# Three gate pairs instead of two computed during the last head, with the branch splits placed among the last two gate slabs

## The chip, the cores and the metric

The kernel runs on one core of a Trainium2 chip. The metric is the device time of one execution in microseconds (us), as a median of several runs. PE is TensorE, the matmul engine (PEld its weight loads), DVE is VectorE, ACT is ScalarE, POOL is GpSimd, SP is SyncE, whose queue issues the loads. Each engine has its own instruction stream, which it works off in order; they meet in semaphores.

## The reference

Two transformer blocks, one after the other, on 512 tokens of width 1024, in 32-bit floats. The place of this change is the end of the first block's mixer:

```
u = rmsnorm(x, norm_mix_g);  proj = u @ w_in        # q, k, v, z of 8 delta-rule heads, fq, fk, fv of 8 attention heads,
                                                    # gate_a and gate_b, 1024 columns each
y_a = branch_a @ w_proj_gdn                         # branch_a: the 8 delta-rule heads, normed and gated, 1024 wide
y_b = branch_b @ w_proj_fox                         # branch_b: the 8 attention heads, 1024 wide
merged = sigmoid(gate_a) * y_a + sigmoid(gate_b) * y_b
h = x + merged @ w_out
x = h + square(relu(rmsnorm(h) @ w_up)) @ w_down
```

The second block has the same ending (retention and windowed attention as branches, biases on the gates, a merge, an output projection, a gated MLP).

## The kernel before, in words

Activations lie transposed: features on the 128 partitions, 512 tokens along a row. A tensor of 1024 features is 8 tiles of 128x512, numbered k. Weights come as 302 **slabs** of 1024x128 (512 KB), each of which gives 128 output features: `load_slab` on SP's queue into one of four slots, `split_hi` on ACT (rounded to the fast matmul type), `split_lo` on POOL (the remainder, in two pieces), and `slab_products` on PE: for each k three matmuls of 128x512, high by high, high by low, low by high (lines 284 to 286), 24 for a slab, all into one bank of PSUM. Both factors need the two parts, so activations are split in the same way.

`ORDER` is an order written out by hand for one round of the heads, a list of tokens that every engine walks: `s3.1` is part k=1 of the round's slab 3, `e3` is the emptying of slab 3's bank by DVE (times the row of norms), the others are stages of the head before. At `sj.0` ACT and POOL split slab j+2 (`LEAD = 2`). Rounds 1 to 7 are a loop. The last round, `LAST`, has no next head to project, so it carries the stages of head 7 and, spread among them, 2 x `AHEAD` = 4 gate slabs: gate_a and gate_b for merge tiles 0 and 1. Their 32 parts are dealt out over the 56 places of a full round. They go to buffers that the heads don't need any more (`gates_ahead`).

Then comes the merge, `merge_tiles`: a tile m makes 128 output features of `merged`. The first `AHEAD` tiles are written out and have two slabs each (j = 2, 3: the two branch projections, into banks bA and bB); the others are a loop and have four (j = 0, 1: the two gates, then the branches). PE waits before j = 2 of every tile until DVE has taken both branch results of the tile before (`branch_taken`, 2q+1). ACT takes the tanh of the ready gates and splits the slabs two ahead, both behind a wait for the tile before (`merged`).

Before the merge the two branches must be split as well. ACT waits for `branches_done`, a one-column instruction of DVE behind the last head's results, then copies 16 tiles to the high parts (`branches_hi`, line 540); DVE subtracts 16 times (`branches_lo`, line 546). The first tile's first two slabs wait for these slice by slice:

```
for k in range(KT):
    if first:
        pe.wait_ge(sem("br_lo"), 2 * KT * rnd + 2 * k + j - 1)
    slab_products(pe, ph, i, slabs[j], (bA, bB)[j - 2][:], (a_hi, b_hi)[j - 2], (a_lo, b_lo)[j - 2], ks=(k,))
```

The second block does the same with `ORDER2`, a last round of 8 gate slabs (`AHEAD2 = 4`) and four merge tiles with ready gates.

Of the kernel before, what the change touches and what calls it, by code (L numbers as in the profile page):

```python
# [23 lines left out]
F32 = mybir.dt.float32  # L24
F32R = mybir.dt.float32r

P = 128
T = 512
NT = T // P
D = 1024  # L30
KT = D // P
EPS = 1e-6
HEADS = 8
# [5 lines left out]
DVE_STEPS, LATE_STEPS = 26, 10  # L39
LEAD = 2  # L40

AHEAD = 2
AHEAD2 = 4
RET_HEADS = 4
FF2_TILES = 22
# [88 lines left out]
def program(nc, dram, out):  # L134
    order = slab_order()

    ph_heads = Phase(7, HEADS)
    ph_gates = Phase(2 * AHEAD, 1, ph_heads)
# [17 lines left out]
    with ExitStack() as ctx:  # L156
# [55 lines left out]
        gains = small("gains", [P, 5, KT])  # L212
        sq_sum = small("sq_sum", [P, T])
        r_row = small("r_row", [P, T])
        r_diag = small("r_diag", [P, NT, P])
        ms_col = small("ms_col", [P, NT])
        r_col = small("r_col", [P, NT])
        head_gain = small("head_gain", [P, 3])
# [8 lines left out]
        def sem(name):  # L227
            if name not in sems:
                sems[name] = ctx.enter_context(nc.semaphore(name))
            return sems[name]  # L230
# [101 lines left out]
        head.at = 183 * KiB  # L332
        rawq = [head(f"raw_qkv{n}", [P, 3 + T]) for n in range(3)]
        raw_fq, raw_fk, raw_fv = [head(f"raw_{n}", [P, T]) for n in ("fq", "fk", "fv")]
        gates_ahead = [rawq[0][:, 3:3 + T], rawq[1][:, 3:3 + T], rawq[2][:, 3:3 + T], raw_fq[:], raw_fk[:], raw_fv[:]]

        pre = Bump(80 * KiB, 112 * KiB)
        x_tok = pre("x_tok", [P, NT, D])
# [35 lines left out]
        LAST, places, part = [], [n for n, t in enumerate(ORDER) if is_slab(t)], 0  # L374
        for n, t in enumerate(ORDER):
            if n in places:
                if (places.index(n) + 1) * 2 * AHEAD * KT // len(places) > part:
                    LAST.append(f"s{part // KT}.{part % KT}")
                    if part % KT == 0 and part:
                        LAST.append(f"e{part // KT - 1}")  # L380
                    part += 1
            elif t not in LATE and not is_evac(t):
                LAST.append(t)
        LAST.append(f"e{2 * AHEAD - 1}")
        FIRST = [t for t in ORDER if is_slab(t) or is_evac(t) or t in LATE]
        FIRST.remove("tq")
# [145 lines left out]

        merge_g = mtmp

        def branches_hi(act, rnd):

            act.wait_ge(sem("branches_done"), rnd + 1)
            for k in range(KT):
                for hi, br in ((a_hi, br_a), (b_hi, br_b)):
                    act.copy(hi[:, k, :], br[:, k, :]).then_inc(sem("br_hi"), 1)  # L540

        def branches_lo(dve, rnd):
            for k in range(KT):
                for n, (hi, lo, br) in enumerate(((a_hi, a_lo, br_a), (b_hi, b_lo, br_b))):
                    dve.wait_ge(sem("br_hi"), (rnd * KT + k) * 2 + n + 1)
                    dve.tensor_tensor(lo[:, k, :], br[:, k, :], hi[:, k, :].bitcast(F32), ALU.subtract)\  # L546
                        .then_inc(sem("br_lo"), 1)


        def gates_before(rnd, m):  # L550
# [28 lines left out]
            merge_tiles(pe, phs, rnd, tile)  # L579

        def merge_act(act, phs, rnd):
            branches_hi(act, rnd)

            def tile(ph, i, slabs, m, ahead):
                q = rnd * KT + m
                if ahead:
                    if rnd == 0:
                        act.wait_ge(s_taken, 7 * HEADS + 2 * m + 2)
                    else:
                        act.wait_ge(sem("taken2"), ph_kv.n + 8 * (RET_HEADS - 1) + 2 * m + 2)  # L590
                    act.wait_ge(sem("merged"), 3 * q + 1)
                    for j in range(2):
                        src = gates_ahead[2 * m + j] if rnd == 0 else h_res[:, 2 * m + j, :]
                        act.activation(merge_g[j][:], src, ACT.Tanh, scale=0.5).then_inc(sem("gate_tanh"), 1)
                        split_hi(act, ph, i, slabs[2 + j] + LEAD)
                    if rnd == 1 and m == AHEAD2 - 1:
                        act.wait_ge(sem("gate_tanh"), 2 * q + 2)
                        act.dma_start(h_res[:].rearrange("p k t -> p (k t)"), h_store[:, :]).then_inc(sem("ld_x"), 16)
                    return
                for j in range(4):  # L600
                    split_hi(act, ph, i, slabs[j] + LEAD)
                    if j < 2:
                        act.wait_ge(sem("gate_taken"), gates_before(rnd, m) + j + 1)
                        act.activation(merge_g[j][:], merge_g[j][:], ACT.Tanh, scale=0.5).then_inc(sem("gate_tanh"), 1)  # L604
            merge_tiles(act, phs, rnd, tile)
# [228 lines left out]
        def ret_rounds(eng, per_round):  # L834

            per_round(FIRST2, ph_kv, 0, None)
            with eng.Fori(0, RET_HEADS - 1) as i:
                per_round(ORDER2, ph_ret, i, i)
            per_round(ORDER2, ph_gates2, 0, RET_HEADS - 1)

        L_BANKS = [(bC, bD), (bE, bF)]

# [125 lines left out]
        def ret_act(act):  # L968
# [7 lines left out]
            def per_round(tokens, ph, i, c):  # L976
# [62 lines left out]
                def ev(a_):  # L1039
                    act.wait_ge(sem("att_t_ps"), 2 * c + a_ + 1)  # L1040
                    act.copy(br_b[:, bass.ds(2 * c + a_, 1), :].rearrange("p a t -> p (a t)"), bB[:])\
                        .then_inc(sem("att_out"), 1)
# [3 lines left out]
                for a_ in range(2):  # L1046
                    stages[f"swa{a_}"] = lambda a_=a_: swa(a_)
                    stages[f"ev{a_}"] = lambda a_=a_: ev(a_)
                for u in range(4):
                    stages[f"E{u}"] = lambda u=u: softmax(u)  # L1050
                    stages[f"T{u}"] = lambda u=u: probs_t(u)
# [5 lines left out]
        def ret_dve(dve, step):  # L1057
# [10 lines left out]
            def per_round(tokens, ph, i, c):  # L1068
# [124 lines left out]
                def on2(a_):  # L1193
                    dve.wait_ge(sem("o2_ps"), 4 * c + 2 * a_ + 2)
                    dve.wait_ge(sem("att_inv"), 4 * c + 2 * a_ + 2)
                    if a_ == 0:
                        dve.wait_ge(sem("sp_ps"), 3 * c + 3)
                    else:
                        dve.wait_ge(sem("att_t_ps"), 2 * c + 1)
                    dve.tensor_tensor(a_out[:].rearrange("p (m d) -> p m d", d=64),  # L1200
                                      bA[:].rearrange("p (m d) -> p m d", d=64),
                                      rd2[:].rearrange("p n u -> p (n u)").unsqueeze(2).to_broadcast([P, 2 * NT, 64]),
                                      ALU.mult).then_inc(sem("att_scaled"), 1)
# [5 lines left out]
                for a_ in range(2):  # L1209
                    stages[f"ra{a_}"] = lambda a_=a_: rota(a_)  # L1210
                    stages[f"on{a_}"] = lambda a_=a_: on2(a_)
                for u in range(4):
                    stages[f"lg{u}"] = lambda u=u: logits(u)
                    stages[f"M{u}"] = lambda u=u: sums(u)
# [9 lines left out]
                    assert step.n == RET_STEPS, step.n  # L1224
            ret_rounds(dve, per_round)
            step.straight(start[0] + RET_HEADS * RET_STEPS)
            dve.wait_ge(sem("ret_out"), 2 * RET_HEADS)
            dve.wait_ge(sem("att_out"), 2 * RET_HEADS + 1)
            dve.tensor_scalar(ms_col[:], ms_col[:], 1.0, None, ALU.mult).then_inc(sem("branches_done"), 1)

        def ret_pool(pool):
            def per_round(tokens, ph, i, c):
# [135 lines left out]
            ffn_pool(pool)  # L1368

        def after_heads_dve(dve, step):  # L1370
            dve.wait_ge(sem("oa"), HEADS)
            dve.wait_ge(sem("ob"), HEADS)
            dve.tensor_scalar(ms_col[:, 0:1], ms_col[:, 0:1], 1.0, None, ALU.mult).then_inc(sem("branches_done"), 1)
            branches_lo(dve, 0)
            merge_dve(dve, (ph_merge0, ph_merge1), 0)
            out_dve(dve, ph_out1, 1, 32)
            mlp_dve(dve)
            ret_dve(dve, step)
            branches_lo(dve, 1)
            merge_dve(dve, (ph_merge2a, ph_merge2), 1, bias_gate)  # L1380
            out_dve(dve, ph_out2, 3, 48)
            ffn_dve(dve)
# [284 lines left out]
        def _(act):  # L1667
# [11 lines left out]
            def head_round(tokens, i, c):  # L1679
# [112 lines left out]
                for n in range(NT):  # L1792
                    stages[f"E{n}"] = lambda n=n: probs(n)
                    stages[f"T{n}"] = lambda n=n: probs_t(n)
                    stages[f"O{n}"] = lambda n=n: outs(n)
                run(tokens, stages, slab, None)

            head_rounds(act, head_round)
# [4 lines left out]
        def _(dve):  # L1803
# [15 lines left out]
            def head_round(tokens, i, c):  # L1819
# [5 lines left out]
                def evac(j):  # L1825
                    dst = (rawq[0], rawq[1], rawq[2], raw_fq, raw_fk, raw_fv, raw_z)[j]
                    dst = dst[:, 3:3 + T] if j < 3 else dst[:]
                    dve.wait_ge(s_used, ph.index(ph_i, j) + 1)
                    if c is not None and j == 5:
                        dve.wait_ge(sem("fvt_ps"), c + 1)  # L1830
                    dve.tensor_tensor(dst, slab_bank(i, j)[:], r_row[:], ALU.mult).then_inc(s_taken, 1)

# [219 lines left out]
                def probs(i_):  # L2052
# [7 lines left out]
                          "gates1": gates1, "gates2": gates2, "cola": cola, "colb": colb, "colh": colh, "dif": dif,  # L2060
                          "bd": bd, "dm": dm, "qd": qd, "fk": fk, "kpd": kpd, "vp": vp_, "kk": kk, "qk": qk, "z0": z0,
                          "xt": xt, "vk": vk, "osq": osq, "on": on_, "oa": oa}
                for x in range(4):
                    stages[f"sl{x}"] = lambda x=x: silu(x)
                for x in range(3):
# [159 lines left out]
```

## Time and profile before

| | us |
|---|---|
| median of 3 runs | 2073.38 (2070.56 to 2073.69) |
| the profiled execution | 2072.55 |
| its span in the trace | 2070.8 |
| PE busy in it | 1995.8 |
| granted TensorE clock, mean | 0.99 |

The span is measured in the trace, from the first to the last instruction; the device time of the same execution has 1.75 us around it. Matmuls overlap in the records: one of 128x512 is shown as about 390 ns, and the next starts some 230 ns after it, so paces are read from start to start. "issue" as a releaser means that the profile shows nothing for which the engine waited.

### The profile page before, as it was taken

What the parts mean: (1) busy time and instruction counts of PE and PEld (TensorE: products, weight loads), DVE (VectorE), ACT (ScalarE), POOL (GpSimd) and SP (SyncE); (2) the same over time, 40 slices, a digit from 0 to 9 for tenths busy, and PEclk for the clock granted to TensorE, in tenths of its full rate; (3) what the DMA queues carried; (4) which work ended last, traced back from release to release, by engine and by line L of the source; (5) the groups of instructions that cost most, each with busy time, mean ns of one, the idle gap of its engine ahead of it and who ended that gap; (6) DMA issues with size and microseconds to landing.
All of it is one profiled execution on the core that took longest, in us unless ns stands there. A gap on an engine that the chain in (4) does not pass through costs nothing.

```text
span 2070.8 us, 29716 instructions
## 1 busy us (share of the span) xinstructions
PE 1995.8 (96%) x11060; PEld 1630.5 (79%) x11060; DVE 909.3 (44%) x1578; ACT 691.5 (33%) x1390; POOL 929.1 (45%) x711
## 2 busy tenths in 40 slices
PE   6999999999989999999999999999989999999997
PEld 5788778887768888888888777777768888888886
DVE  4666776667642222121212355655642324335143
ACT  4333333333342223332324343444332233223222
POOL 3443344434425456444445533333325456545455
PEclk9999999999999999999999999999999999999998
DMA  5111111111113252333323321121124323323332
GB/s 184 62 62 53 57 42 61 61 51 51 61 42 106 87 176 92 102 93 101 101 91 93 112 81 61 61 61 61 51 72 133 110 72 102 111 82 93 101 102 71
DMA packets 50646, 174.25 MB, mean 84 GB/s; under 512 B 6544, under 2 KB 7312, under 8 KB 50320
## 3 DMA queue, kind: packets, MB, share of 16 engines
q1 hardware_dynamic: 50432, 171.20, 25.8%
q10 hardware_dynamic: 144, 2.10, 0.3%
q8 instruction: 47, 0.77, 0.1%
q14 instruction: 23, 0.19, 0.0%
HBM read 169.08 MB, written 4.19 MB: 84 GB/s over the span
## 4 chain that ended last, share of the span: by engine, by line
PE 88%; DVE 7%; ACT 2%; issue 2%; DMA 0%; POOL 0%; DVEq 0%; POOLq 0%; ACTq 0%; SPq 0%
PE bank L284 25%; PE bank L286 24%; PE bank L285 24%; PE bank L1458 3%; PE bank L1447 2%; PE bank L1441 2%; PE bank L944 1%; PE bank L1640 1%; DVE att_neg_max L1182 1%; PE bank L1627 1%; DVE ret_g_raw L1157 1%; PE bank L914 1%; DVE branch_a_lo L546 0%; DVE decay_b L1938 0%; DVE att_logits L1178 0%
## 5 line engine op out<-in xcount | busy, mean ns | idle before, releaser
L273 POOL TENSOR_TENSOR slab_lo<-slab_raw,slab_hi 128x512 fp32r<-128x512 f32 x604 | 821.5, 1385 | 1015.5 <-ACT slab_hi L266 1015.4
L284 PE MATMUL bank<-u_hi,slab_hi 128*128 128x512 f32 x1584 | 658.4, 416 | 17.9 <-POOL slab_lo L273 13.5
L286 PE MATMUL bank<-u_hi,slab_lo 128*128 128x512 f32 x1584 | 622.3, 393 | 0.0
L285 PE MATMUL bank<-u_lo,slab_hi 128*128 128x512 f32 x1584 | 621.2, 392 | 0.0
L266 ACT CAST slab_hi<-slab_raw 128x1024 fp32r<-128x1024 f32 x302 | 314.1, 1046 | 231.6 <-PE bank L286 230.6
L284 PEld LDWEIGHTS bank<-u_hi,slab_hi 128*128 128x128 f32 x1584 | 300.2, 189 | 80.3 <-issue 18.2
L286 PEld LDWEIGHTS bank<-u_hi,slab_lo 128*128 128x128 f32 x1584 | 299.3, 189 | 65.1
L285 PEld LDWEIGHTS bank<-u_lo,slab_hi 128*128 128x128 f32 x1584 | 300.7, 190 | 53.9 <-issue 1.7
L284 PE MATMUL bank<-hidden_hi,slab_hi 128*128 128x512 f32 x432 | 168.4, 390 | 0.3
L285 PE MATMUL bank<-hidden_lo,slab_hi 128*128 128x512 f32 x432 | 168.1, 389 | 0.0
L286 PE MATMUL bank<-hidden_hi,slab_lo 128*128 128x512 f32 x432 | 168.1, 389 | 0.0
L482 DVE TENSOR_TENSOR residual<-residual,bank 128x512 f32<-128x512 f32 x48 | 33.0, 688 | 200.6 <-PE bank L286 200.6
L284 PEld LDWEIGHTS bank<-hidden_hi,slab_hi 128*128 128x128 f32 x432 | 81.1, 188 | 18.4 <-DVE residual L1326 1.6
L286 PEld LDWEIGHTS bank<-hidden_hi,slab_lo 128*128 128x128 f32 x432 | 81.1, 188 | 16.8
L285 PEld LDWEIGHTS bank<-hidden_lo,slab_hi 128*128 128x128 f32 x432 | 81.1, 188 | 16.7
L634 DVE SCALAR_TENSOR_TENSOR mtmp<-mtmp,bank 128x512 f32<-128x512 f32 x32 | 22.0, 688 | 138.6 <-PE bank L286 138.6
L1291 ACT ACTIVATE tmp<-tmp 128x512 f32<-128x512 f32 x22 | 13.9, 632 | 177.7 <-DVE tmp L1312 177.7
L284 PE MATMUL bank<-branch_a_hi,slab_hi 128*128 128x512 f32 x128 | 52.7, 412 | 10.1 <-issue 8.4
L604 ACT ACTIVATE mtmp<-mtmp 128x512 f32<-128x512 f32 x20 | 12.6, 632 | 145.9 <-DVE mtmp L623 86.0
L765 DVE SCALAR_TENSOR_TENSOR tmp<-bank,r_row 128x512 f32<-128x512 f32 x32 | 22.1, 692 | 85.0 <-PE bank L286 85.0
L1326 DVE TENSOR_TENSOR residual<-residual,bank 128x512 f32<-128x512 f32 x24 | 16.5, 688 | 94.8 <-PE bank L286 94.8
L736 ACT ACTIVATE tmp<-tmp 128x512 f32<-128x512 f32 x32 | 20.2, 632 | 110.1 <-DVE tmp L765 110.1
(342 smaller groups left out, 2727.4 us busy)
## 6 DMA issues: line engine op xcount, KB each, us to landing
slab_raw<-slabs SPq DMA_DIRECT2D x302, 512.0 KB, 3.5
residual<-x_t SPq DMA_DIRECT2D x2, 1024.0 KB, 7.2
x_tok<-x SPq DMA_DIRECT2D x1, 2048.0 KB, 12.7
residual<-x_t SPq DMA_DIRECT2D x1, 2048.0 KB, 8.9
residual_store<-residual SPq DMA_DIRECT2D x1, 2048.0 KB, 8.7
residual<-residual_store ACTq DMA_DIRECT2D x1, 2048.0 KB, 8.1
out_t<-residual SPq DMA_DIRECT2D x8, 256.0 KB, 2.1
cos_ret<-cos_r SPq DMA_DIRECT2D x1, 256.0 KB, 3.7
```

Source lines behind the costliest of these rows:

```text
L266: act.copy(w_hi[s][:], raw[s][:]).then_inc(s_hi, 1)
L273: ins = pool.tensor_tensor(w_lo[s][:, ks, :], raw[s][:, ks, :], w_hi[s][:, ks, :].bitcast(F32), ALU.subtract)
L284: pe.matmul(bank, w_hi[s][:, k, :], x_hi[:, k, :], start=first, stop=False)
L285: pe.matmul(bank, w_hi[s][:, k, :], x_lo[:, k, :], start=False, stop=False)
L286: mm = pe.matmul(bank, w_lo[s][:, k, :], x_hi[:, k, :], start=False, stop=last)
L482: ins = dve.tensor_tensor(h_res[:, m, :], h_res[:, m, :], bank[:], ALU.add)
L634: dve.scalar_tensor_tensor(out=merge_g[j][:], in0=merge_g[j][:], scalar=1.0, in1=(bA, bB)[j][:], op0=ALU.add, op1=ALU.mult).then_inc(sem(" ...
L765: dve.scalar_tensor_tensor(out=tmp[j % 2][:], in0=bank_slab[j % 2][:], scalar=0.0, in1=r_row[:], op0=ALU.max, op1=ALU.mult).then_inc(sem(" ...
L914: mm = pe.matmul(L_BANKS[u][b // 2][:, at_ + (P if b == 0 else 0):at_ + 2 * P], a_q[a_][half, b * P:(b + 1) * P], k_cur[half, k0:(b + 1) * P],
L1441: mm = pe.matmul(out_[:, c], lhs[:, c], rhs[:, c], start=start, stop=stop)
L1447: mm = pe.transpose(out_[:, c], in_[:, c], ident[:])
L1458: mm = pe.matmul(out_[r, c], lhs[r, c], rhs[r, c], start=True, stop=True)
```

## The change

`AHEAD` goes from 2 to 3, so that three pairs of gate slabs are computed in the last round, and three merge tiles are written out with two slabs each; the loop has five turns in place of six. The list of slabs in memory follows. `SPREAD = 4` keeps the first four gate slabs on the places that they had; gate slabs 4 and 5 stand behind the emptying of the fourth, and among their sixteen parts stand eight new tokens `br0` to `br7`. Each is one k of the branch splits: two copies on ACT (`branch_hi`), two subtractions on DVE (`branch_lo`); the wait for the heads' results and the one-column instruction are in front of k = 0. PE has no such stage. The third pair goes to `sq_sum` and to a new buffer, which takes the place of one that was not used. In the second block the eight tokens stand behind all of the last round.

```diff
-AHEAD = 2
+AHEAD, SPREAD = 3, 4
...
-        r_diag = small("r_diag", [P, NT, P])
+        spare_g = small("spare_gate", [P, T])
...
-        gates_ahead = [rawq[0][:, 3:3 + T], rawq[1][:, 3:3 + T], rawq[2][:, 3:3 + T], raw_fq[:], raw_fk[:], raw_fv[:]]
+        gates_ahead = [rawq[0][:, 3:3 + T], rawq[1][:, 3:3 + T], rawq[2][:, 3:3 + T], raw_fq[:], sq_sum[:],
+                       spare_g[:]]
...
-                if (places.index(n) + 1) * 2 * AHEAD * KT // len(places) > part:
+                if (places.index(n) + 1) * SPREAD * KT // len(places) > part:
...
+        LAST.append(f"e{SPREAD - 1}")
+        for g in range((2 * AHEAD - SPREAD) * KT):
+            j, t = SPREAD + g // KT, g % KT
+            LAST.append(f"s{j}.{t}")
+            if t == 0 and j > SPREAD:
+                LAST.append(f"e{j - 1}")
+            if g % 2 == 0:
+                LAST.append(f"br{g // 2}")
         LAST.append(f"e{2 * AHEAD - 1}")
...
-        def branches_hi(act, rnd):
-
-            act.wait_ge(sem("branches_done"), rnd + 1)
-            for k in range(KT):
-                for hi, br in ((a_hi, br_a), (b_hi, br_b)):
-                    act.copy(hi[:, k, :], br[:, k, :]).then_inc(sem("br_hi"), 1)
...
+        def branch_hi(act, rnd, k):
+
+            if k == 0:
+                act.wait_ge(sem("branches_done"), rnd + 1)
+            for hi, br in ((a_hi, br_a), (b_hi, br_b)):
+                act.copy(hi[:, k, :], br[:, k, :]).then_inc(sem("br_hi"), 1)
+
+        def branch_lo(dve, rnd, k):
+            if k == 0:
+                if rnd == 0:
+                    dve.wait_ge(sem("oa"), HEADS)
+                    dve.wait_ge(sem("ob"), HEADS)
+                else:
+                    dve.wait_ge(sem("ret_out"), 2 * RET_HEADS)
+                    dve.wait_ge(sem("att_out"), 2 * RET_HEADS + 1)
+                dve.tensor_scalar(ms_col[:, 0:1], ms_col[:, 0:1], 1.0, None, ALU.mult).then_inc(sem("branches_done"), 1)
+            for n, (hi, lo, br) in enumerate(((a_hi, a_lo, br_a), (b_hi, b_lo, br_b))):
+                dve.wait_ge(sem("br_hi"), (rnd * KT + k) * 2 + n + 1)
+                dve.tensor_tensor(lo[:, k, :], br[:, k, :], hi[:, k, :].bitcast(F32), ALU.subtract)\
+                    .then_inc(sem("br_lo"), 1)
...
         def merge_act(act, phs, rnd):
-            branches_hi(act, rnd)
-
...
-            per_round(ORDER2, ph_gates2, 0, RET_HEADS - 1)
+            per_round(ORDER2 + [f"br{k}" for k in range(KT)], ph_gates2, 0, RET_HEADS - 1)
...
                     dve.wait_ge(s_used, ph.index(ph_i, j) + 1)
-                    if c is not None and j == 5:
+                    if ph is ph_heads and c is not None and j == 5:
                         dve.wait_ge(sem("fvt_ps"), c + 1)
```

The calls of `branches_hi` and `branches_lo` and the one-column instructions ahead of them go away in both blocks; the stage tables of ACT and DVE get `br0` to `br7`.

## Rows read from the trace of the kernel before

**Rows 1.** The page: span, and busy time, share and instructions of each engine.
```profile
span 2070.8 us, 29716 instructions
...
PE 1995.8 (96%) x11060; PEld 1630.5 (79%) x11060; DVE 909.3 (44%) x1578; ACT 691.5 (33%) x1390; POOL 929.1 (45%) x711
```

**Rows 2.** The chain of waits, 580 to 640: start, us, what.
```profile
599.73 0.63 ACT branch_a_hi L540
600.38 0.69 DVE branch_a_lo L546
...
609.56 0.50 PE bank L284
```

**Rows 3.** Timeline around the first merge: start, us, engine, line [idle before, releaser].
```profile
597.83 0.40 PE L286 MATMUL bank<-u_hi,slab_lo 128*128 128x512 f32 x1
...
598.52 0.39 PE L286 MATMUL bank<-u_hi,slab_lo 128*128 128x512 f32 x1
598.94 0.69 DVE L1831 TENSOR_TENSOR raw_fq<-bank,r_row 128x512 f32<-128x512 f32 x1 [2.01 <-PE bank L286]
599.55 0.14 DVE L1373 TENSOR_SCALAR ms_col<-ms_col 128x1 f32<-128x1 f32 x1
600.25 0.61 ACT L540 CAST branch_b_hi<-branch_b 128x512 fp32r<-128x512 f32 x1
...
601.17 0.47 PE L284 MATMUL bank<-branch_a_hi,slab_hi 128*128 128x512 f32 x1 [2.27 <-issue]
...
602.92 0.63 PE L285 MATMUL bank<-branch_a_lo,slab_hi 128*128 128x512 f32 x1
603.35 0.63 PE L286 MATMUL bank<-branch_a_hi,slab_lo 128*128 128x512 f32 x1
...
609.42 0.69 DVE L546 TENSOR_TENSOR branch_b_lo<-branch_b,branch_b_hi 128x512 fp32r<-128x512 f32 x1
...
610.36 0.39 PE L284 MATMUL bank<-branch_b_hi,slab_hi 128*128 128x512 f32 x1
```

**Rows 4.** The same timeline where merge tile 1 follows tile 0.
```profile
615.59 0.39 PE L286 MATMUL bank<-branch_b_hi,slab_lo 128*128 128x512 f32 x1
...
616.80 0.47 PE L284 MATMUL bank<-branch_a_hi,slab_hi 128*128 128x512 f32 x1 [0.83 <-issue]
...
617.34 0.40 PE L286 MATMUL bank<-branch_a_hi,slab_lo 128*128 128x512 f32 x1
...
619.25 1.04 ACT L266 CAST slab_hi<-slab_raw 128x1024 fp32r<-128x1024 f32 x1
...
620.36 3.80 POOL L273 TENSOR_TENSOR slab_lo<-slab_raw,slab_hi 128x512 fp32r<-128x512 f32 x3 [5.34 <-ACT slab_hi L266]
```

**Rows 5.** Groups by line, DVE then ACT, 596 to 611: busy, mean ns, idle before.
```profile
L546 DVE TENSOR_TENSOR branch_a_lo<-branch_a,branch_a_hi 128x512 fp32r<-128x512 f32 x8 | 5.5, 686 | 0.7 <-ACT branch_a_hi L540 0.7
...
L266 ACT CAST slab_hi<-slab_raw 128x1024 fp32r<-128x1024 f32 x2 | 2.1, 1034 | 0.0
```

**Rows 6.** Windows: busy PE, PEld, DVE, ACT, POOL; granted clock, DMA share, GB/s.
```profile
598.90:610.36 11.46, 8.25 (x25) 5.18 (x25) 10.48 (x18) 10.63 (x20) 0.66 (x1) 0.85 0.00 0
...
627.75:650.00 22.25, 22.25 (x100) 18.40 (x98) 4.74 (x8) 5.15 (x6) 10.22 (x9) 1.00 0.33 109
```

**Rows 7.** Timeline of the last head: POOL's pieces of the last slab split there.
```profile
585.54 2.52 POOL L273 TENSOR_TENSOR slab_lo<-slab_raw,slab_hi 128x512 fp32r<-128x512 f32 x2 [3.53 <-ACT slab_hi L266]
```

**Rows 8.** The chain of waits in the second merge, 1505 to 1700.
```profile
1526.40 0.83 issue
...
1550.37 0.83 issue
```

**Rows 9.** Timeline: the first matmul of the second merge.
```profile
1511.59 0.47 PE L284 MATMUL bank<-branch_a_hi,slab_hi 128*128 128x512 f32 x1 [2.80 <-issue]
```

**Rows 10.** POOL's slab pieces, 575 to 612 (ns min/median/max), and the timeline around one.
```profile
L273 POOL TENSOR_TENSOR slab_lo<-slab_raw,slab_hi x6: 1273/1285/1572, 579.5 to 611.2; 128x512 fp32r<-128x512 f32 x6
...
609.70 5.32 POOL L273 TENSOR_TENSOR slab_lo<-slab_raw,slab_hi 128x512 fp32r<-128x512 f32 x4 [14.99 <-ACT slab_hi L266]
```

More of the change, by code:

```diff
@@ L533, in program @@
         merge_g = mtmp
-        def branches_hi(act, rnd):
-            act.wait_ge(sem("branches_done"), rnd + 1)
-            for k in range(KT):
-                for hi, br in ((a_hi, br_a), (b_hi, br_b)):
-                    act.copy(hi[:, k, :], br[:, k, :]).then_inc(sem("br_hi"), 1)
[L542 to L547, printed above, removed]
+        def branch_hi(act, rnd, k):
[16 more added lines that the diff above has]
+                    .then_inc(sem("br_lo"), 1)
         def gates_before(rnd, m):
@@ L1048, in per_round @@
                     stages[f"ev{a_}"] = lambda a_=a_: ev(a_)
+                for k in range(KT):
+                    stages[f"br{k}"] = lambda k=k: branch_hi(act, 1, k)
                 for u in range(4):
@@ L1211, in per_round @@
                     stages[f"on{a_}"] = lambda a_=a_: on2(a_)
+                for k in range(KT):
+                    stages[f"br{k}"] = lambda k=k: branch_lo(dve, 1, k)
                 for u in range(4):
@@ L1226, in ret_dve @@
             step.straight(start[0] + RET_HEADS * RET_STEPS)
-            dve.wait_ge(sem("ret_out"), 2 * RET_HEADS)
-            dve.wait_ge(sem("att_out"), 2 * RET_HEADS + 1)
-            dve.tensor_scalar(ms_col[:], ms_col[:], 1.0, None, ALU.mult).then_inc(sem("branches_done"), 1)
         def ret_pool(pool):
@@ L1370, in after_heads_dve @@
         def after_heads_dve(dve, step):
[L1371 to L1374, printed above, removed]
             merge_dve(dve, (ph_merge0, ph_merge1), 0)
@@ L1378, in after_heads_dve @@
             ret_dve(dve, step)
-            branches_lo(dve, 1)
             merge_dve(dve, (ph_merge2a, ph_merge2), 1, bias_gate)
@@ L1795, in head_round @@
                     stages[f"O{n}"] = lambda n=n: outs(n)
+                for k in range(KT):
+                    stages[f"br{k}"] = lambda k=k: branch_hi(act, 0, k)
                 run(tokens, stages, slab, None)
@@ L1827, in evac @@
                     dst = dst[:, 3:3 + T] if j < 3 else dst[:]
+                    if ph is ph_gates:
+                        dst = gates_ahead[j]
                     dve.wait_ge(s_used, ph.index(ph_i, j) + 1)
-                    if c is not None and j == 5:
+                    if ph is ph_heads and c is not None and j == 5:
                         dve.wait_ge(sem("fvt_ps"), c + 1)
@@ L2062, in head_round @@
                           "xt": xt, "vk": vk, "osq": osq, "on": on_, "oa": oa}
+                for k in range(KT):
+                    stages[f"br{k}"] = lambda k=k: branch_lo(dve, 0, k)
                 for x in range(4):
```

## The prediction

> **What bounds the kernel now.** I read the page first: the reader is to see one engine, TensorE (PE), busy for 96% of the span, and the other three below half [rows 1]. Busy time on DVE, ACT or POOL is then worth nothing by itself; only places where PE stands still are. The kernel has few. The edited place lies between the last head and the first merge, so I took the chain of waits there: from 599.73, over ACT's first copy and then DVE's subtractions, to 609.56 it leaves PE out [rows 2]. The timeline shows why. The last matmul of the fourth gate slab starts at 598.52; DVE empties its bank (598.94) and writes one column that stands for "branches done" (599.55); only then ACT rounds the first branch tile (599.73), DVE forms its remainder (600.38), and PE can start at 601.17. From there PE multiplies k-slice by k-slice as fast as DVE hands them over: the last slice of this slab starts at 609.56, the next slab at 610.36 [rows 3].
>
> The pace without waits is read behind it: from 610.36 to 615.59 there are 23 matmuls, 5.23 us, so 0.2274 each, 5.46 for a slab of 24 [rows 3, 4]. From 598.52 to 610.36 there are 25 steps, which at that pace take 5.69; they took 11.84. **The stall is 6.15 us.** DVE sets it: 16 subtractions of 0.69, which start 0.60 apart (600.38 to 609.42 in 15 steps), against 0.52 for ACT's 16 copies (599.73 to 600.25) [rows 2, 3, 5]. In the middle PE ran matmuls 0.43 apart (602.92, 603.35) at the lower level of its clock, 1.2 GHz, after the idle time (granted clock of the stretch 0.85); it made that up while DVE went on, since it waits for DVE again at the last slices, so the slow matmuls are inside the 6.15 and not beside it [rows 3, 6].
>
> **The change, part by part.** *Removed from the merge's way:* the 16 copies and 16 subtractions. *Put in their place on PE:* two gate slabs, 48 matmuls that a merge tile in the loop did before. PE's total of matmuls, ACT's, POOL's and DVE's full-size instructions and the slabs loaded all stay what they were; the first four gate slabs keep their 32 places in the last head, since the spread is still over four. Up to 598.75 nothing differs.
>
> *Does the cover hold?* PE needs for slabs five and six only slabs that were split at the tokens two slabs ahead, the later of them done on POOL by 588.06 [rows 7], the bank of slab five, emptied before the fourth slab ends, and that of slab six, which is the fourth slab's and is emptied by 599.63 [rows 3]. So PE runs 598.75 to 609.7. Beside it: "branches done" at 599.7 as before; ACT's first eight copies 599.73 to 603.9, the split of the next slab (1.04 in [rows 5]) to 604.9, eight more copies to 609.1; DVE's first eight subtractions 600.38 to 605.2, the emptying of slab five, which PE has finished at about 604.4, to 605.9, eight more subtractions to about 610.8. The merge's first slab starts at 609.7 and asks for slice 7 after 21 matmuls, at 614.5; the remainder it needs is there at 610.2, 4.3 us earlier. For slice 0 the margin is 8.6. ACT's split of the slab behind it, now queued behind "branches done" and eight copies, gives POOL its work at 604.9; that is done by 607.6 and needed at 615.2. Behind the last copies wait the tanh and the split for the second merge tile: done on POOL by about 613.9, needed at 621.6. Every item has over four microseconds. The queues moved past are SP's too: its loads wait only for POOL's split four slabs before, which now comes earlier for two of them; the residual's reload waits for one more merged tile, but it stands in SP's queue behind all loads of the merge loop and is issued late anyway. I therefore take the whole stall as gone: **-6.15**. If the cover were missing, the 16 subtractions would cost that again.
>
> *Added:* a merge tile whose gates are ready has only two slabs, and the next one starts on the same two banks. PE waits until DVE has emptied the second: from 615.59 to 617.34 three steps take 1.75 in place of 0.68, **1.07 us** [rows 4]. In the loop two gate slabs come between and hide this; PE is busy throughout [rows 6]. Before there is one such join in this merge, after there are two (tile 0 to 1, 1 to 2). The second merge, with four such tiles, shows three joins, the last 23.97 after the first (1526.40, 1550.37), where two tiles of 48 steps take 21.83: the same 1.07 each [rows 8]. Bounds: 0.83, the idle time recorded, and 1.07. I take +1.07.
>
> *Moved matmuls:* in the last head steps run at 0.230 (597.83 to 598.52) against 0.2274 in the merge [rows 3]; 48 of them give **+0.1**, at least 0.
>
> *The rest costs nothing:* gates of pair three go to two other buffers of the same size; the one-column instruction is as before; in the second merge the eight splits stand in the same order behind the last gate's emptying, so its stall of 2.80 before the first matmul and what follows remain [rows 9]. One loop turn less has no price that a row shows, bounded by the 0.00 that PE is idle from 627.75 to 650.00 [rows 6].
>
> Sum: -6.15 + 1.07 + 0.1 = **-5.0 us**. Bounds from these terms: -6.15 + 0.83 = -5.3, and, if the margin failed by half the subtractions, about -2. The profiled execution took 2072.55 (span 2070.8 and 1.75 around it), so 2067.6 by its own time; the median shown is 2073.38, 0.8 above it, which gives 2068.4. I predict 2068.0, between them.
>
> **Rivals.**
> *The cover is partial.* POOL stands idle for 14.99 us around the splits now; afterwards its two pieces for the merge's second slab fall among DVE's subtractions. The one overlap in the trace: the POOL piece that starts at 609.70 beside the subtraction of 609.42 is the long one, 1572 ns against a median of 1285 [rows 3, 10]. If DVE were held for two whole pieces, it would be 2.6 late, inside the margin of 4.3; only with ACT late as well would PE wait, 2 to 3 us in all, for 2070 to 2071. The Trainium skill, "SBUF — State Buffer", section "Who interferes with whom", says that a DVE instruction with two SBUF inputs and a GpSimd instruction that reads SBUF exclude each other for a whole instruction; the row shows 0.29 us lost and on POOL, and by the rule alone the subtractions would end at some 613.4 and the time would still be that of the sum. 0.08.
>
> *The third tile is dearer than the first join.* ACT's splits in such a tile stand behind the tile before it being merged: 619.25, POOL from 620.36, two pieces done by 622.9, needed at 627.75, so 4.8 us of slack [rows 4, 6]. Three such tiles run in the second merge without a wait beyond the join [rows 8], which speaks against it. If the join cost double, the gain would be 4: 2069.4. 0.05.
>
> *Slower.* The same queue, worse: ACT's tanh and split, held behind "branches done" and sixteen copies, reach POOL so late that the slabs for tiles 1 and 2 and for the loop's entry arrive after PE. It decides when the splits of a tile are more than 4.8 us late; to end above the kernel before by 0.2% the stalls must come to 5.0 + 4.1 = 9.1 us, three tiles at 3 us each: 2077. My timeline has the first of these splits ending at 611.2, 10.4 us before its slab is needed, and no load that could delay it. 0.03.
>
> *It does more.* The join is hidden in part or the head's end gets shorter because ACT and POOL split earlier: 2066 to 2067. For it: nothing but the bound of the terms. 0.04.
>
> **How the numbers follow.** The forecast has 0.80. The three runs before lie from 2070.56 to 2073.69, 3.1 us apart, and the result is a median of such runs; about one microsecond either way belongs to any forecast. The range runs from 2065.8 (2068.0 less the noise and the case with more) to 2070.8 (plus the partial cover). A time within 0.2%, 4.1 us, of the one before can't be told from no change. The forecast's gain of 5.0 clears that by only 0.9, which it does in some seven of eight measurements: 0.80 x 0.88 + 0.04 = 0.74 faster. Same is 0.10 + 0.08 + 0.05 = 0.23, slower 0.03.
>
> **What would show it.** Right: 48 more u_hi matmuls directly behind 598.5 with steps of 0.23; DVE's sixteen subtractions start at 600.4 as before, in two groups of eight with an emptying between; the wait of PE for branch_a_lo in the first merge gone, with no idle time of 2.3 before the first merge matmul and no fallen clock there; two idle times of 0.83 in the first merge; the one wait of 2.80 in the second merge unchanged [rows 9]; the end earlier by about 5.0. Wrong: PE waiting before the fifth or sixth slab, or for slab_lo in tiles 1 to 3; the second group of subtractions starting later than 609; a POOL piece or subtraction well over its 1.3 and 0.69 us; any gain given back after the merge, where the trace gives no reason for it.

## The result, and the profile after

The changed kernel is slower: a median of 2082.80 us in five runs (2081.27 to 2084.47), beside 2072.53 for the kernel before (2070.56 to 2073.69); the ratio is 1.0045, with a 95% interval from 1.0034 to 1.0057. The forecast was 5.0 us less; the measured difference is 9 to 10 us more. Timed again in another session the ratio was 1.0039 (1.0026 to 1.0052). The profiled execution took 2082.80, its span is 2081.0.

Its page first, against [rows 1]: PE's busy time grew by 4, the span by 10, and no other engine came near being full.

```profile
span 2081.0 us, 29664 instructions
...
PE 2000.0 (96%) x11060; PEld 1634.6 (79%) x11060; DVE 917.9 (44%) x1578; ACT 691.7 (33%) x1390; POOL 932.5 (45%) x711
```

The waits of PE from 540 to 760 (line waited for: us in total, times, longest) show the place. The wait that the change was to remove is there again, in four pieces of up to 2.4 us.

```profile
PE bank L284 <- DVE branch_a_lo L562: 7.3, 4, 2.4
PE bank L284 <- issue: 1.7, 2, 0.8
```

And the waits of ACT from 590 to 640 show what nobody had asked about before: ACT stood still for 10.9 us, waiting for PE, ahead of the split of a slab.

```profile
ACT mtmp L608 <- DVE merged_lo L657: 17.8, 1, 17.8
ACT slab_hi L266 <- PE bank L286: 11.1, 2, 10.9
```

The timeline of the same place, which answers to [rows 3, 4]: start, us, engine, line, and in brackets the idle time before and what ended it.

```profile
599.25 0.39 PE L286 MATMUL bank<-u_hi,slab_lo 128*128 128x512 f32 x1
...
599.68 0.69 DVE L1845 TENSOR_TENSOR raw_fq<-bank,r_row 128x512 f32<-128x512 f32 x1 [1.99 <-PE bank L286]
600.29 0.14 DVE L559 TENSOR_SCALAR ms_col<-ms_col 128x1 f32<-128x1 f32 x1
605.12 1.05 ACT L266 CAST slab_hi<-slab_raw 128x1024 fp32r<-128x1024 f32 x1 [10.93 <-PE bank L286]
606.07 0.62 ACT L549 CAST branch_a_hi<-branch_a 128x512 fp32r<-128x512 f32 x1
606.25 3.00 POOL L273 TENSOR_TENSOR slab_lo<-slab_raw,slab_hi 128x512 fp32r<-128x512 f32 x2 [10.78 <-ACT slab_hi L266]
606.72 1.37 DVE L562 TENSOR_TENSOR branch_a_lo<-branch_a,branch_a_hi 128x512 fp32r<-128x512 f32 x1 [6.29 <-ACT branch_a_hi L549]
608.01 1.78 DVE L562 TENSOR_TENSOR branch_b_lo<-branch_b,branch_b_hi 128x512 fp32r<-128x512 f32 x1
609.72 0.68 DVE L562 TENSOR_TENSOR branch_a_lo<-branch_a,branch_a_hi 128x512 fp32r<-128x512 f32 x1
...
611.69 3.35 POOL L273 TENSOR_TENSOR slab_lo<-slab_raw,slab_hi 128x512 fp32r<-128x512 f32 x2 [2.44 <-ACT slab_hi L266]
...
617.32 6.85 POOL L273 TENSOR_TENSOR slab_lo<-slab_raw,slab_hi 128x512 fp32r<-128x512 f32 x4 [2.27 <-ACT slab_hi L266]
...
622.97 1.75 DVE L562 TENSOR_TENSOR branch_a_lo<-branch_a,branch_a_hi 128x512 fp32r<-128x512 f32 x1
...
624.77 0.80 PE L284 MATMUL bank<-branch_a_hi,slab_hi 128*128 128x512 f32 x1 [2.40 <-DVE branch_a_lo L562]
...
626.22 0.63 PE L284 MATMUL bank<-branch_b_hi,slab_hi 128*128 128x512 f32 x1
...
633.42 0.39 PE L286 MATMUL bank<-branch_b_hi,slab_lo 128*128 128x512 f32 x1
...
634.64 0.47 PE L284 MATMUL bank<-branch_a_hi,slab_hi 128*128 128x512 f32 x1 [0.83 <-issue]
```

Two things are to be seen. "Branches done" is written at 600.29 (before: 599.55; this whole execution is 0.74 later here), but ACT makes its first copy at 606.07. And where a POOL piece runs beside them, DVE's subtractions take 1.37 to 1.78 us in place of 0.69. The groups of DVE and POOL from 599 to 626 (count, busy us, mean ns) give the sum:

```profile
L562 DVE TENSOR_TENSOR branch_b_lo<-branch_b,branch_b_hi 128x512 fp32r<-128x512 f32 x8 | 9.8, 1226 | 0.0
L562 DVE TENSOR_TENSOR branch_a_lo<-branch_a,branch_a_hi 128x512 fp32r<-128x512 f32 x8 | 9.3, 1166 | 6.3 <-ACT branch_a_hi L549 6.3
...
L273 POOL TENSOR_TENSOR slab_lo<-slab_raw,slab_hi 128x512 fp32r<-128x512 f32 x8 | 13.2, 1673 | 15.5 <-ACT slab_hi L266 15.5
```

The sixteen subtractions took 19.1 us, against 11.0 at 0.687 each [rows 5], and eight POOL pieces averaged 1673 ns against a median of 1285 [rows 10].

The price on PE: from 599.25 to 626.22 lie 73 steps, which at the pace of 0.2274 take 16.6; they took 26.97, so 10.4 were lost. The next slab (626.22 to 633.42, 23 steps) took 7.2 in place of 5.2, because the clock had fallen to its lower level, 1.2 GHz, for part of it (steps 0.43 apart up to 630.05); the windows (last columns: granted clock, DMA share, GB/s) show a mean of 0.70:

```profile
599.00:625.79 26.79, 19.50 (x75) 14.35 (x73) 19.82 (x20) 13.37 (x22) 13.21 (x8) 0.90 0.13 39
625.79:633.42 7.63, 7.63 (x25) 6.11 (x24) 0.81 (x2) 0.00 (x0) 0.00 (x0) 0.70 0.01 2
```

Together 12.3 against the 6.15 of the kernel before, and one join more at 1.07: the first merge should be 7.3 later. For a check without any pace, I take in each kernel the time between two events that all of them have: the emptying of the fourth gate slab's bank (598.94 before, 599.68 after) and the issue of the residual's store behind the first block (1175.1 and 1183.2). It is 576.17 before and 583.48 after: **+7.3**. This distance is used for every experiment below, and the last column of the table is worked out in the same way, from times to a hundredth.

### The profile page after: what moved, and what is told of

Read it like the earlier page. It is cut to its first block, busy times and chain, and to the rows that moved or that the text cites. A ratio compares the mean times of both kernels' runs of the same rounds, so it can differ in the third digit from the quotient of the medians.

```text
span 2081.0 us, 29664 instructions
## 1 busy us (share of the span) xinstructions
PE 2000.0 (96%) x11060; PEld 1634.6 (79%) x11060; DVE 917.9 (44%) x1578; ACT 691.7 (33%) x1390; POOL 932.5 (45%) x711
## 4 chain that ended last, share of the span: by engine, by line
PE 87%; DVE 8%; ACT 2%; issue 2%; DMA 0%; POOL 0%; DVEq 0%; POOLq 0%; ACTq 0%; SPq 0%
PE bank L284 25%; PE bank L286 24%; PE bank L285 24%; PE bank L1468 3%; PE bank L1457 2%; PE bank L1451 2%; PE bank L958 1%; PE bank L1650 1%; DVE att_neg_max L1198 1%; PE bank L1637 1%; DVE branch_a_lo L562 1%; DVE branch_b_lo L562 1%; DVE ret_g_raw L1173 0%; DVE decay_b L1952 0%; DVE att_logits L1194 0%
## 5 line engine op out<-in xcount | busy, mean ns | idle before, releaser
L474 POOL TENSOR_TENSOR sq_sum<-sq_sum,mtmp 128x512 f32<-128x512 f32 x27 | 35.0, 1295 | 47.5 <-ACT mtmp L465 47.5
```

The source lines that it names most:

```text
L474: pool.tensor_tensor(sq_sum[:], sq_sum[:], mtmp[m % 2][:], ALU.add).then_inc(sem("norm_sum"), 1)
```

## The experiments

Two theories went in. *Slots:* a phase of slabs always begins in slot 0. The gate phase now has six slabs and ends in slot 1, so the merge's first slab (slab 6) lies in slot 0, that of slab 4, two slabs earlier and not four. ACT's split of slab 6 must wait until PE is through with slab 4, and the eight copies stand behind it in ACT's queue. *Port:* DVE's subtraction, which reads two tiles of SBUF, and POOL's slab piece, which reads SBUF too, hold each other up.

| kernel | device time, us | ratio to before (95%) | distance, us | against before |
|---|---|---|---|---|
| before | | | 576.2 | |
| changed | 2082.80 | 1.0045 (1.0034 to 1.0057) | 583.5 | +7.3 |
| changed, again | 2081.16 | 1.0039 (1.0026 to 1.0052) | 583.0 | +6.9 |
| slots continued | 2068.17 | 0.9974 (0.9964 to 0.9984) | 571.1 | -5.1 |
| POOL light | 2071.26 | 0.9993 (0.9984 to 1.0003) | 572.6 | -3.6 |
| splits late | 2074.73 | 1.0012 (1.0003 to 1.0022) | 579.1 | +3.0 |
| splits late, slots continued | 2072.19 | 0.9998 (0.9986 to 1.0011) | 577.3 | +1.1 |
| copies ahead of the slab splits | 2066.56 | 0.9968 (0.9955 to 0.9980) | 571.1 | -5.1 |
| before, POOL reads beside | 2084.69 (one run) | | 588.0 | +11.8 |
| before, POOL writes beside | 2071.17 (one run) | | 576.1 | 0.0 |
| slots continued, two bank pairs | 2060.94 | 0.9944 (0.9931 to 0.9957) | 568.9 | -7.3 |
| the same, second tail interleaved | 2059.79 | 0.9934 (0.9918 to 0.9950) | 568.9 | -7.3 |

The kernel before had medians of 2072.34 to 2073.99 in these sessions.

**Slots continued.** The phases get a first slot; the merge's first phase starts where the gates ended.

```diff
-        return (j % self.n) % SLOTS
+        if self.then and j >= self.n:
+            return self.then.slot(j - self.n)
+        return (j % self.n + self.shift) % SLOTS
...
-    ph_merge0 = Phase(2 * AHEAD, 1, ph_gates)
+    ph_merge0 = Phase(2 * AHEAD, 1, ph_gates, 2 * AHEAD % SLOTS)
     ph_merge1 = Phase(4, KT - AHEAD, ph_merge0)
+    ph_gates.then, ph_merge0.then = ph_merge0, ph_merge1
```

> The changed kernel with one thing undone: the first merge phase starts in slot 2, where the six gate slabs end, so that every slab again reuses the slot of the slab four before it. Slot theory (ACT stood at the split of slab 6 until PE had finished slab 4, 10.9 us idle, because both lie in slot 0): ACT's copies start at once behind branches-done, some 6 us earlier, the splits end before PE needs them, and the time is 5 us below the kernel before, 2067 to 2069. Port theory (DVE's subtractions and POOL's pieces exclude each other, and that alone eats the cover): the subtractions still take 1.7 us wherever POOL works, the stream still needs 18 us instead of 10 and PE waits 4 us or more: 2072 or above.

2068.17, as the slot theory had it. The timeline of this kernel:

```profile
599.23 0.62 ACT L556 CAST branch_a_hi<-branch_a 128x512 fp32r<-128x512 f32 x1 [5.37 <-DVE ms_col L566]
...
604.11 0.68 DVE L569 TENSOR_TENSOR branch_b_lo<-branch_b,branch_b_hi 128x512 fp32r<-128x512 f32 x1
604.53 3.12 POOL L280 TENSOR_TENSOR slab_lo<-slab_raw,slab_hi 128x512 fp32r<-128x512 f32 x2 [7.84 <-ACT slab_hi L273]
604.71 0.68 DVE L1852 TENSOR_TENSOR sq_sum<-bank,r_row 128x512 f32<-128x512 f32 x1
605.31 1.19 DVE L569 TENSOR_TENSOR branch_a_lo<-branch_a,branch_a_hi 128x512 fp32r<-128x512 f32 x1
606.42 1.78 DVE L569 TENSOR_TENSOR branch_b_lo<-branch_b,branch_b_hi 128x512 fp32r<-128x512 f32 x1
```

ACT copies right behind "branches done". The long subtractions are still there, but only four (1.19, 1.78, and 1.79 and 1.77 later), since POOL did slab 6 before them; they end at 614.0, in time, and PE waits for none. Its waits from 598 to 760 are the two joins:

```profile
PE bank L291 <- issue: 1.7, 2, 0.8
```

The port alone costs nothing here, which is also how the sum had it.

**POOL light.** The changed kernel, where POOL's pieces have 8 of 128 columns. The expectation says slabs 6 to 9; the edit takes all six slabs of the merge's first phase, 6 to 11. The last two are split when the subtractions are over, so the reading of the first merge slab is the same.

```diff
+            some = P
+            if (ph is ph_gates and j >= ph.n) or (ph is ph_merge0 and j < 6):
+                some = 8
...
-                ins = pool.tensor_tensor(w_lo[s][:, ks, :], raw[s][:, ks, :], w_hi[s][:, ks, :].bitcast(F32),
+                ins = pool.tensor_tensor(w_lo[s][:, ks, 0:some], raw[s][:, ks, 0:some], w_hi[s][:, ks, 0:some].bitcast(F32),
```

> The changed kernel, where POOL forms the low parts of slabs 6 to 9 behind the last head (the first four of the merge) for 8 of 128 columns only; the rest of those low parts is left out. Slots as in the changed kernel. Port theory: no subtraction of DVE is longer than 0.7 us; the stream, though it starts 6 us late at 606.7, takes 10.5 us plus the wait for ACT's split of slab 7, and PE waits at most 2 us: 2068 to 2071. Slot theory alone: the late start is what costs, so PE still waits most of what it waits now and the time stays near 2080.

ACT stood still as long as in the changed kernel (10.96 us) and DVE began at 607.12, but every subtraction took 0.68 or 0.69:

```profile
605.51 1.05 ACT L266 CAST slab_hi<-slab_raw 128x1024 fp32r<-128x1024 f32 x1 [10.96 <-PE bank L289]
606.64 0.46 POOL L276 TENSOR_TENSOR slab_lo<-slab_raw,slab_hi 128x32 fp32r<-128x32 f32 x2 [10.81 <-ACT slab_hi L266]
607.12 0.69 DVE L565 TENSOR_TENSOR branch_a_lo<-branch_a,branch_a_hi 128x512 fp32r<-128x512 f32 x1 [6.29 <-ACT branch_a_hi L552]
607.73 0.68 DVE L565 TENSOR_TENSOR branch_b_lo<-branch_b,branch_b_hi 128x512 fp32r<-128x512 f32 x1
```

2071.26, 0.3 above the expected range, refutes the slots as the only cause: with the late start alone the distance is 1.5 us above that of the kernel with continued slots (572.6 and 571.1). So each cause without the other is nearly harmless, and both together cost 12.4 (583.5 and 571.1). They multiply: the wait ahead of the copies pushes slab 6's POOL pieces, and later those of slabs 8 and 9, in among the subtractions, eight pieces in place of four, each of which delays DVE by up to 1.1 us.

**Splits late**, with the slots of the changed kernel and with continued ones. The eight tokens stand behind the last emptying.

```diff
-            if g % 2 == 0:
-                LAST.append(f"br{g // 2}")
         LAST.append(f"e{2 * AHEAD - 1}")
+        LAST += [f"br{k}" for k in range(KT)]
```

> The changed kernel with the eight branch-split tokens behind the emptying of the last gate slab instead of among the two last slabs. Slot theory: ACT reaches the copies only after slab 5 is finished (it must split slab 7, whose slot is slab 5's), at about 611.7, 1.5 us after PE; the whole stall of 6.15 us of the kernel before comes back, 1.5 more, one join more at 1.07: 2075 to 2076. Port theory adds up to 1.1 us for each subtraction beside POOL's two pieces of slab 7: up to 2079. If interleaving were the harm, it would be near the 2073 of the kernel before.

> Both edits: slots that continue as in the first experiment, and the branch splits behind all gate slabs. What is left of the change is the third written-out tile. The stall of 6.15 us is as in the kernel before, POOL has done its pieces by then, and the one join more costs 1.07 us: 1 us above the kernel before, 2073 to 2075. If the join has no price: equal to it. If the third pair costs something that I have not seen (its buffers, the shorter loop), more than 2 us above it.

With continued slots the distance is 1.1 above the kernel before: the third written-out tile costs its one join and nothing else. With the short slots it is 1.9 more; two subtractions are long (1.34 and 1.77), beside POOL's pieces of slab 7. Later in the same stream the meeting ends the other way round: POOL's next piece takes 3.30, and the subtractions beside it keep their time.

```profile
619.84 3.30 POOL L273 TENSOR_TENSOR slab_lo<-slab_raw,slab_hi 128x512 fp32r<-128x512 f32 x1 [6.83 <-ACT slab_hi L266]
620.10 0.68 DVE L561 TENSOR_TENSOR branch_b_lo<-branch_b,branch_b_hi 128x512 fp32r<-128x512 f32 x1
620.71 0.68 DVE L561 TENSOR_TENSOR branch_a_lo<-branch_a,branch_a_hi 128x512 fp32r<-128x512 f32 x1
```

The device times, 2074.73 and 2072.19, lie 0.3 and 0.8 below their expected ranges, and the second's interval reaches from 2.9 below to 2.3 above the kernel before, so the join is read from the distance.

**POOL beside the splits of the kernel before.** One instruction, eight times, started with the copies, each waiting for the one before it.

```diff
+            if rnd == 0:
+                pool.wait_ge(sem("branches_done"), 1)
+                for n in range(8):
+                    pool.tensor_tensor(r_diag[:].rearrange("p n c -> p (n c)"), r_row[:], r_row[:], ALU.subtract).then_inc(sem("pool_extra"), 1)
+                    pool.wait_ge(sem("pool_extra"), n + 1)
```

> The kernel before, with eight extra POOL subtractions of 128x512 (both inputs one SBUF tile, output into the unused buffer) started together with the branch splits, where POOL was idle. Port theory: the 1.77 us subtractions of DVE appear beside them, as many as POOL has pieces, each 1.1 us longer than 0.69, and the stall of the first merge grows by 5 us or more: 2078 or above. If the long subtractions of the changed kernel had another cause (PE's matmuls on u_hi, the loads, ACT's copies), DVE stays at 0.69 and the time at 2073.

The subtractions became long one after the other, and the first merge 11.8 us longer, with no slab or slot touched. Twelve of the sixteen are long, not eight: eight beside the added instructions (0.98, then 1.52 or 1.53), and four (1.74 or 1.75) beside the slab pieces that POOL starts at 611.74, into which the delay had pushed them.

```profile
600.49 11.16 POOL L611 TENSOR_TENSOR r_diag<-r_row 128x512 f32<-128x512 f32 x8 [5.07 <-DVE ms_col L1379]
...
602.00 1.53 DVE L546 TENSOR_TENSOR branch_b_lo<-branch_b,branch_b_hi 128x512 fp32r<-128x512 f32 x1
603.45 1.52 DVE L546 TENSOR_TENSOR branch_a_lo<-branch_a,branch_a_hi 128x512 fp32r<-128x512 f32 x1
```

In the other kernel POOL's instruction is `pool.memset(r_diag..., 0.0)`, which writes the same tile and reads nothing.

> As the kernel before with eight extra POOL instructions beside the branch splits, but these only write (the unused buffer is set to zero, nothing is read). If what holds DVE is POOL reading SBUF while DVE reads two SBUF operands, the subtractions stay at 0.69 beside them and the first merge's stall at 6.15: 2073. If any POOL instruction holds DVE, the subtractions are long as in the run in which POOL reads.

```profile
600.04 4.60 POOL L611 MEMSET r_diag<- 128x512 f32 x8 [5.02 <-DVE ms_col L1379]
...
601.27 0.68 DVE L546 TENSOR_TENSOR branch_b_lo<-branch_b,branch_b_hi 128x512 fp32r<-128x512 f32 x1
601.87 0.69 DVE L546 TENSOR_TENSOR branch_a_lo<-branch_a,branch_a_hi 128x512 fp32r<-128x512 f32 x1
```

The distance is that of the kernel before to a tenth. Of these two instructions the one that reads holds DVE and the one that only writes does not, so the Trainium skill's sentence in "SBUF — State Buffer", section "Who interferes with whom", agrees with this case: a DVE instruction with two SBUF inputs contends with a GpSimd instruction that reads SBUF and not with one that only writes.

**Copies ahead of the slab splits.** The changed kernel with its short slots; only the order of tokens differs. PE's stream is the same.

```diff
+        LAST += [f"br{k}" for k in range(4)] + ["s4.0", "e4"] + [f"br{k}" for k in range(4, 8)]
+        LAST += [f"s4.{t}" for t in range(1, KT)] + [f"s5.{t}" for t in range(KT)] + ["e5"]
```

> The changed kernel with its short slot distance, but with ACT's copies br0 to br3 ahead of the split of slab 6 and br4 to br7 ahead of the split of slab 7 (both splits must wait for PE, until about 605 and 610.5, and ACT copies in that time in place of standing still). If the slots hurt only because ACT's queue stands still in front of the copies, DVE's first eight subtractions start at 600.4 at 0.69 each, two to four later ones are long, PE waits at most 2 us: 2068 to 2071. If the late split of slabs 6 and 7 itself (its low part late for PE) or POOL's pieces are what costs, it stays above 2075.

2066.56, which is 1.4 below the expected range, and the distance of the kernel with continued slots:

```profile
599.45 0.62 ACT L543 CAST branch_a_hi<-branch_a 128x512 fp32r<-128x512 f32 x1 [6.31 <-DVE ms_col L553]
...
604.11 1.05 ACT L266 CAST slab_hi<-slab_raw 128x1024 fp32r<-128x1024 f32 x1 [0.38 <-PE bank L286]
...
610.68 8.81 POOL L273 TENSOR_TENSOR slab_lo<-slab_raw,slab_hi 128x512 fp32r<-128x512 f32 x6 [2.45 <-ACT slab_hi L266]
614.52 0.68 DVE L1839 TENSOR_TENSOR spare_gate<-bank,r_row 128x512 f32<-128x512 f32 x1
```

The split of slab 6 still waits for PE, until 604.11, but nothing stands behind it that is needed earlier. Four subtractions are long, as with continued slots. So the short distance by itself costs nothing either, here or at the entry of the merge loop, where slab 12 reuses the slot of slab 10; what costs is the blocked split at the head of ACT's queue in front of the copies.

**The changed kernel again, and two further versions.** The joins can go: merge tiles whose gates are ready use two pairs of banks in turn, and PE waits for the tile before the last.

```diff
+        def pair(m, ahead):
+            return (bC, bD) if ahead and m % 2 else (bA, bB)
...
-                    pe.wait_ge(sem("branch_taken"), 2 * q + 1)
+                    pe.wait_ge(sem("branch_taken"), 2 * q - 1 if ahead and m else 2 * q + 1)
```

> The changed kernel once more, beside the others on one chip. Up to the store of the residual after the first block it lay 8.1 us behind the kernel before, 7.4 of them in the first merge; the rest of the 10 us came in the second block's head rounds, where the granted clock fell at other places (rounds of 72 us at full clock, 74 to 75.6 with falls, in every kernel here). If that rest is chance, the first part is again +8 within 1 us in the profile and the whole lies anywhere between 7 and 11 above the kernel before. If it belongs to the change, it is again +10.

The whole, 7.2 above the kernel before, lies in the expected span. The distance grew by 6.9, as in the first profile within 0.5. At the residual's store itself the kernel was only 5.6 behind (1180.7 and 1175.1), not 8, because this execution reached the emptying of the fourth gate slab 1.2 earlier (597.69 and 598.94).

> The changed kernel with continued slots (first experiment) and with the merge tiles whose gates are ready on two pairs of banks in turn, so that PE waits for the results of the tile before the last only. If the join of 1.07 us is the wait for the two banks, all five joins (two in the first merge, three in the second) go: 5.3 us below the first experiment, 10 to 11 below the kernel before, 2062 to 2064. If the join is something else (the wait for the low part of the next slab, or a start-up of PE), the idle times of 0.83 stay and the time is that of the first experiment, 2068.

With continued slots and two pairs the idle times of 0.83 are gone in both merges, and the distance falls by another 2.2, two joins at 1.07. 2060.94 is 13 us below the kernel before, 2 to 3 more than the 10 to 11 forecast. The interval, 8.9 to 14.3, contains the forecast, and where the excess comes from is open.

The last version puts the splits of the second block among the last five parts of its last gate slab.

```diff
-            per_round(ORDER2 + [f"br{k}" for k in range(KT)], ph_gates2, 0, RET_HEADS - 1)
+            cut = ORDER2.index("ev1") + 1
+            end = [t for n, p in enumerate(ORDER2[cut:-1]) for t in (p, f"br{n}")]
+            end += [f"br{k}" for k in range(len(end) // 2, KT)] + ORDER2[-1:]
+            per_round(ORDER2[:cut] + end, ph_gates2, 0, RET_HEADS - 1)
```

> As the second, and in the second block the branch splits start behind the last stage that reads their buffers, among the last five parts of the last gate slab (its bank is emptied after them), in place of behind all of it. Slot-and-cover theory: five parts of 0.68 us of PE's work lie beside them, so 3 to 4 us less than the second kernel, 2059 to 2061, and POOL has no pieces there that could lengthen the subtractions. If the stages before them end later than those parts, nothing is gained: equal to the second kernel.

In its trace the part from the start of the last score products of the second block's heads to the reload of the residual takes 94.7 us, against 97.6 in the version before it: the 3 us are there. The medians, 2059.79 and 2060.94, do not tell the two apart; its six runs spread from 2054.3 to 2065.0.

**What stays open.** In the first session 9.3 us were lost (7.0 to 11.8), and the first block explains 7.3. The rest lies in the head rounds of the second block, whose code the change does not touch. Their length differs between executions with the granted clock. Three windows, one round each, of the kernel with late splits and of the one with late splits and continued slots:

```profile
1236.90:1309.10 72.20, 66.45 (x366) 55.07 (x365) 43.84 (x85) 32.06 (x73) 23.44 (x17) 1.00 0.18 59
```

```profile
1235.80:1311.40 75.60, 69.90 (x366) 57.99 (x365) 42.74 (x84) 32.34 (x73) 22.98 (x17) 0.95 0.17 56
1311.40:1387.00 75.60, 69.88 (x365) 57.94 (x364) 42.52 (x84) 32.27 (x73) 22.97 (x17) 0.95 0.16 55
```

The three loop rounds together took 219.8 us before, 222.9 and 225.9 in the two profiles of the changed kernel, and 218.2 to 225.8 in the others, without an order that follows any of the edits. Whether the changed kernel draws such rounds more often than chance was not settled: the interval of the second session, 5.4 to 10.8 us, contains 7.

## Why the prediction was wrong

**The stall, the pace and the join were right.** With continued slots PE waits for no subtraction and the distance falls by 5.1, against the forecast's 5.0; the join of 1.07 was measured alone (+1.1), and taken away (-2.2 for two).

**The step that failed is "Does the cover hold?"** It put ACT's first eight copies at 599.73 to 603.9. The token `s4.0`, with the split of slab 6, stands ahead of `br0` in ACT's queue; the working passed over it as done and had listed only the waits of PE and the split of slab 7. Its wait could be read in the code: `back()` gives slab 6 the slab of the same slot before it, and with six slabs in a phase of four slots that is slab 4. The copies came 5.6 us later than forecast, taking off the 0.74 by which this execution was late. The sentence on SP's queue looked at the loads, which wait for POOL's split of the slab in the same slot; ACT's split waits for something else, that slab's use by PE, and that was not looked up. For the loads "four slabs before" was wrong in the same way: for slabs 6 and 7 it is two.

**The port was weighed, for the wrong timeline.** One overlap was read, with 0.29 us lost on POOL, and the worst case was set at two whole pieces, 2.6 us. It measured 8.1 (19.1 less 11.0). Per piece the estimate was of the right size; the number of pieces was four times too small. With continued slots, where the timeline is the one of the forecast, there are four long subtractions, which is still twice the two pieces, but the last of them is not needed early: the remainder for slice 7 of the first slab is ready at 612.3 (the subtraction of 1.79 that starts at 610.53), and PE takes that slice at 613.88. Of the 4.3 us of margin 1.6 were left. So the bound of 2.6 held for what PE waits for, and the late start had used up the margin by which the prediction set aside the rule of the Trainium skill that it quotes ("SBUF — State Buffer", section "Who interferes with whom").

**The rivals.** The one on the slower side named ACT's queue, but the wrong order: slab splits held behind the copies, where the copies are held behind a slab split. It asked for 9.1 us of stalls and gave it 0.03. The partial cover, at 2070 to 2071, was the nearest in kind: it names ACT late together with DVE held. It stopped at 3 us because it counted two pieces of POOL, and did not ask how many more a late start would bring in. The range ended at 2070.8, 12 us below the result.

**The clock.** It was to be whole; it fell instead after PE had waited between single slices (the longest recorded wait is 2.40), and 2 us of the loss are matmuls of the next slab at the lower level.

## What to carry to other kernels

When the number of steps in a phase changes, write down for each step which earlier one it reuses a buffer of: a ring that starts anew with each phase keeps its full depth only where the phase's length is a multiple of that depth, and here six slabs in four slots halved it for the first two slabs of the next phase. When work is put into a queue, list what stands ahead of it as well as behind it, with each wait; the remedy was to put the tokens of the copies ahead of the two slab splits that must wait, and it gave the whole 5 us that the change was meant to bring. A margin in a timeline is shared by all causes that may use it: two delays that are harmless alone can move each other's work into overlap.

## What the runs showed of the hardware

A DVE subtraction of 128x512 with both inputs in SBUF takes 0.69 us alone and 1.52 to 1.79 beside POOL instructions that read SBUF, less where the overlap is partial (0.98 to 1.37); POOL's piece goes from 1.26 to as much as 1.82. In most meetings both lose: beside slab pieces the long subtractions start 1.66 to 1.71 apart in place of 0.60, which is longer than POOL's 1.26 and shorter than both together. Not in all: in the kernel with late splits one POOL piece took 3.30 and the four subtractions that overlap it kept 0.68. Which side loses was not settled. DVE instructions with one input in PSUM keep their 0.68 beside a busy POOL (the emptying at 614.52 above, while POOL works from 610.68 to 619.49), and a POOL memset of the same tile, 0.58 us, leaves the subtractions at 0.69. Rounds of the same code in the second block last 72.2 us at a granted clock of 1.00 and 75.6 at 0.95, so a gain or loss of a few microseconds in one profile of this kernel says little until the place has been read.
